# State space over spans of eight tokens, first norm in rows, and one reciprocal for sixteen heads' norms

## The reference

```python
h = rms_norm(x, mix_norm_g[layer])
proj = h @ w_in[layer]
u, q, k, v, f_logit, g_ssm, g_att = jnp.split(proj, IN_SPLITS, axis=-1)
y_ssm = s5_branch(u, ...)              # the state space
y_att = forgetting_attention(q, k, v, f_logit, ...)   # q and k get a norm per head
merged = jax.nn.sigmoid(g_ssm) * y_ssm + jax.nn.sigmoid(g_att) * y_att
x = x + merged @ w_out[layer]
```

```python
xr = jnp.einsum('blgh,gph->blgp', ug, br)     # and xi with bi
_, _, sr, si = lax.associative_scan(_complex_affine_combine, (lr, li, xr, xi), axis=1)
y = einsum(sr, c_re) - einsum(si, c_im) + d_skip * u
y = jax.nn.gelu(y); z = y @ w_glu             # then val * sigmoid(gate)
```

## Time and profile before

| | us |
|---|---|
| median of 3 runs | 4165.3 (4160.1 to 4167.3) |
| the profiled execution | 4165.7 |
| its span, first to last instruction | 4164.0 |
| PE busy | 3616.0 (87%) |
| GpSimd busy | 1846.4 (44%) |
| DVE busy | 2298.1 (55%) |
| ACT busy | 1454.7 (35%) |

### The profile page before, as it was taken

How to read it: one execution, slowest core, us unless ns; L and a number is a source line. 1 busy time by engine, 2 the same in 40 slices (tenths; PEclk the granted TensorE clock), 3 DMA queues, 4 the chain that set the end, 5 groups by cost and what they waited for, 6 DMA issues and landing times. The chain is left out here.

```text
span 4164.0 us, 51122 instructions
## 1 busy us (share of the span) xinstructions
PE 3616.0 (87%) x16437; PEld 2823.8 (68%) x16441; DVE 2298.1 (55%) x3833; ACT 1454.7 (35%) x2639; POOL 1846.4 (44%) x994
## 2 busy tenths in 40 slices
PE   7679889555699999999998885899998779989998
PEld 4546677445588888888887553668776554457876
DVE  5977325886498989898994357421102335531101
ACT  5124433177533333333332232433212114433322
POOL 1522342199787888788882110124342200024432
PEclk9889999767799999999999897999998869999999
DMA  3121232012577777777772110123223120012321
GB/s 88 51 73 27 58 97 73 11 81 98 194 267 267 268 267 271 268 265 264 268 272 66 53 42 26 31 66 95 78 83 77 52 77 19 8 56 86 94 76 62
DMA packets 430783, 486.52 MB, mean 117 GB/s; under 512 B 61344, under 2 KB 373952, under 8 KB 412496
## 3 DMA queue, kind: packets, MB, share of 16 engines
q1 hardware_dynamic: 412240, 350.98, 28.3%
q0 software_dynamic: 18432, 134.23, 8.1%
HBM read 448.35 MB, written 29.36 MB: 115 GB/s over the span
## 5 line engine op out<-in xcount | busy, mean ns | idle before, releaser
L124 POOL TENSOR_TENSOR w_low<-w_ring,w_high 128x1024 fp32r<-128x1024 f32 (+2 forms) x264 | 647.6, 2460 | 1675.9 <-ACT w_high L119 1675.9
L135 PE MATMUL ps<-h_low,w_high 128*128 128x512 f32 x1600 | 653.5, 408 | 161.1 <-POOL w_low L124 129.8
L136 PE MATMUL ps<-h_high,w_high 128*128 128x512 f32 x1600 | 640.0, 400 | 0.0
L137 PE MATMUL ps<-h_high,w_low 128*128 128x512 f32 x1600 | 638.7, 399 | 0.0
L135 PEld LDWEIGHTS ps<-h_low,w_high 128*128 128x128 f32 x1600 | 306.9, 192 | 255.6 <-POOL w_low L124 145.3
L124 POOL TENSOR_TENSOR u_low<-w_ring,u_high 128x1024 fp32r<-128x1024 f32 x128 | 366.4, 2862 | 136.8 <-ACT u_high L119 136.3
L119 ACT ACTIVATE w_high<-w_ring 128x1024 fp32r<-128x1024 f32 (+2 forms) x264 | 263.1, 1012 | 301.1 <-PE ps L137 254.1
L124 POOL TENSOR_TENSOR v_low<-v_raw,v_high 128x1024 fp32r<-128x1024 f32 x128 | 348.8, 2725 | 43.2 <-ACT v_high L119 43.2
L136 PEld LDWEIGHTS ps<-h_high,w_high 128*128 128x128 f32 x1600 | 307.4, 192 | 72.3 <-issue 3.6
L137 PEld LDWEIGHTS ps<-h_high,w_low 128*128 128x128 f32 x1600 | 306.7, 192 | 72.8
L135 PE MATMUL ps<-h_low,u_high 128*128 128x384 f32 x1024 | 345.1, 337 | 5.8 <-POOL u_low L124 5.8
(11 more groups left out here) (406 smaller groups left out, 7165.1 us busy)
## 6 DMA issues: line engine op xcount, KB each, us to landing
w_ring<-in_peer_uT_dram SPq DMA_DIRECT2D x128, 512.0 KB, 7.6
v_raw<-in_peer_uv_dram SPq DMA_DIRECT2D x128, 512.0 KB, 4.5
peer_gates<-ring SPq DMA_DIRECT2D x12, 2048.0 KB, 6.2
gates<-peer_gates SPq DMA_DIRECT2D x32, 768.0 KB, 9.5
w_ring<-in_ffn_w_gate_dram SPq DMA_DIRECT2D x44, 512.0 KB, 3.8
w_ring<-in_ffn_w_up_dram SPq DMA_DIRECT2D x44, 512.0 KB, 3.8
w_ring<-in_w_in_dram SPq DMA_DIRECT2D x36, 512.0 KB, 3.9
w_ring<-in_ffn_w_down_dram SPq DMA_DIRECT2D x32, 448.0 KB, 3.7
```

Source lines behind the costliest of these rows:

```text
L124: return eng.tensor_tensor(rounded(low), whole, high, ALU.subtract)
L135: nc.tensor.matmul(out, rounded(w_high), rounded(x_low), start=start, stop=False, **more)
L136: nc.tensor.matmul(out, rounded(w_high), rounded(x_high), start=False, stop=False, **more)
L137: return nc.tensor.matmul(out, rounded(w_low), rounded(x_high), start=False, stop=stop, **more)
```

## The change

The state space works on spans of eight tokens. u is copied out by phases (token mod 8), stored to DRAM and read back so that one partition range holds eight phases of a group's 16 channels. Three kinds of product take the place of fill and read-out over 512 tokens: `reachT` carries the eight inputs of a span into its state, a Toeplitz matrix (`toeplitz`, with the skip on its diagonal) gives what inputs of a span do to outputs of the same span, and `carry` gives what the state before the span does. The scan runs over 64 spans in six levels, all pairs at once. The tables are made by DVE from powers 0 to 8 of lambda. y leaves through DRAM and comes back in phases, and merge reads it by a strided view.

`project` gets a hook `between`: work of an engine after a given turn of its loop. Fill stands after turn 0, the band's DMAs (issued by ACT) after turn 3, read-out and gelu after turn 5. `load_consts` is gone; its loads stand first in the new stage `entry`, whose norm works on x in rows (one sum and one scale per partition). `c.xT` is made after the u projection from the rows and stays in place. The heads' norm gathers its 16 sums in 16 rows of one bank, takes one root and one reciprocal of 16x512, and spreads each row over 128 partitions by a product of halves.

The diff, cut to its core:

```diff
-def project(c, w, evacuate, rhs=None, ahead=None, whole=None, before={}, after={}, norm=None):
+def project(c, w, evacuate, rhs=None, ahead=None, whole=None, before={}, after={}, norm=None, between={}):
...
+    def pieces(eng, name, body, last):
+        at = 0
+        for stop in sorted(between):
+            turn_loop(eng, body, at, stop)
+            if name in between[stop]:
+                between[stop][name](eng)
+            at = stop
+        turn_loop(eng, body, at, last)
...
+    def square(self, act):
+        for t in range(TT):
+            act.wait_ge(self.x_in[t], 16)
...
+            self.c.nc.scalar.activation(self.squares, self.rows[:, t, :], ACT.Square, accum_out=self.total[:, t:t + 1]).then_inc(self.squared, 1)
...
+    def sum(self, pe):
+        pe.wait_ge(self.masks_set, 2)
+        spin(self.c, 7, 16)
...
+        for k in range(KD):
+            if k >= 4:
+                pe.wait_ge(self.low, k - 3)
+            for t in range(TT):
+                tr = self.c.nc.tensor.transpose(self.c.ps[:, 4 + k % 4, t * P:(t + 1) * P], self.scaled[:, t, k * P:(k + 1) * P], self.c.ident[:, :])
+            tr.then_inc(self.turned, 1)
...
+        def load_first(sp):
+            sp.dma_start(c.ident[:, :], c.ins["c_ident"]).then_inc(consts_in, 16)
+            sp.dma_start(c.causal[:, :], c.ins["c_causal"]).then_inc(consts_in, 16)
+            for two in range(2):
+                sp.dma_start(m["dt"][two * SSM_S:(two + 1) * SSM_S, :], dt2[two].partition_broadcast(SSM_S), allow_slow_non_contiguous=True).then_inc(param_in, 16)
+            sp.dma_start(m["ar"][:, :], by_state(A["ssm_a_re"][0]), allow_slow_non_contiguous=True).then_inc(param_in, 16)
+            sp.dma_start(m["ai"][:, :], by_state(A["ssm_a_im"][0]), allow_slow_non_contiguous=True).then_inc(param_in, 16)
+            norm.load_x(sp)
+            for x, name in enumerate(("ssm_b_re", "ssm_b_im")):
+                sp.dma_start(b_in[x][:, :, :], A[name][0].rearrange("(j two) s h -> (two s) j h", two=2)).then_inc(rows_in, 16)
...
+        def turn(pe):
+            for n in range(GROUPS):
...
+        def store_u(sp):
+            for b in range(SSM_T):
+                sp.wait_ge(u_out, b + 1)
+                sp.dma_start(u_dram[b, :, :], tb.phases[:, b, :]).then_inc(u_saved, 16)
+            sp.wait_ge(u_saved, 16 * SSM_T)
+            by_group = u_dram.rearrange("t (g h) (r s) -> r h (t g) s", h=SSM_H, r=PH)
+            for r in range(PH):
+                at = (PH - 1 - r) * SSM_H
+                sp.dma_start(tb.u[at:at + SSM_H, :, :], by_group[r]).then_inc(tb.u_in, 16)
...
+        def fill(pe):
+            pe.wait_ge(tb.u_in, 16 * PH)
+            for x in range(2):
+                for p in range(PAIRS):
+                    for two in range(2):
+                        mm = nc.tensor.matmul(c.ps[HALF[two], 2 + 2 * x + p // 8, p % 8 * SPANS:(p % 8 + 1) * SPANS],
+                                              tb.reachT[:, x, p, HALF[two]], tb.u[:, 2 * p + two, :], start=True, stop=True)
...
+            for p in range(PAIRS):
+                for x in range(2):
+                    for two, half in enumerate(HALF):
+                        mm = nc.tensor.matmul(c.ps[:, 6 + two, p * SSM_H:(p + 1) * SSM_H], tb.reach[half, x, p, :], tb.c[x][half, p, :], start=x == 0, stop=x == 1)
...
+        def band(act):
+            act.wait_ge(cleared, 1)
+            act.wait_ge(diagonal, 2)
+            for r in range(PH):
+                at = (PH - 1 - r) * SSM_H
+                act.dma_start(tb.toeplitz[at:P, r, :], tb.kernel[0:P - at, :, :].rearrange("p h g -> p (h g)")).then_inc(banded, 16)
+
+        def outputs(pe):
+            pe.wait_ge(banded, 16 * PH)
...
+            for p in range(PAIRS):
...
+                for two in range(2):
+                    g = 2 * p + two
+                    nc.tensor.matmul(out[two], toeplitz[:, g::SSM_G], tb.u[:, g, :], start=True, stop=False, skip_group_check=True)
+                for x in range(2):
+                    for two, half in enumerate(HALF):
+                        mm = nc.tensor.matmul(out[two][:, 1:SPANS], carry[half, x, p, :], tb.S[x][half, p, 0:SPANS - 1], start=False, stop=x == 1, skip_group_check=True)
...
+        def load_y(sp):
+            sp.wait_ge(y_saved, 16 * 4)
+            by_channel = y_dram.rearrange("(r h) (t g) s -> g t h r s", h=SSM_H, g=8)
             for g in range(8):
...
+                for t in range(SSM_T):
+                    sp.dma_start(ygT[g * SSM_H:(g + 1) * SSM_H, t, :].rearrange("p (r s) -> p r s", r=PH), by_channel[g, t]).then_inc(yg_in, 16)
...
         def sweeps(dve):
...
+            for x, (first, second, op) in enumerate((((0, 0), (1, 1), ALU.add), ((1, 0), (0, 1), ALU.subtract))):
+                step.mark(v.tensor_tensor(made[x], taps[first[0]], power[first[1]], ALU.mult))
+                step.mark(v.tensor_tensor(part, taps[second[0]], power[second[1]], ALU.mult))
+                step.wait()
+                step.mark(v.tensor_tensor(made[x], made[x], part, op))
+                step.wait()
...
-            for first in range(0, PAIRS, TOGETHER):
-                dve.wait_ge(moved, 2 * (first + TOGETHER))
-                for level in range(BIG):
-                    pair_steps(first, level, False)
...
+            dve.wait_ge(moved, 4)
+            for level in range(LEVELS):
                 all_step(level, False)
...
+            dve.wait_ge(kernel_out, 2)
+            v.memset(tb.toeplitz, 0.0).then_inc(cleared, 1)
...
+        project_copy(c, w_qk, qkT, ahead, before={"dve": sweeps}, after={"sp": load_y},
+                     between={1: {"pe": fill, "act": move}, 4: {"act": band}, 6: {"pe": outputs, "act": gelus}})
...
-                nc.vector.reciprocal(rstd[:, n % ring, :], rstd[:, n % ring, :]).then_inc(inverted, 1)
...
+            v.reciprocal(rstd[:, :], rstd[:, :]).then_inc(inverted, 1)
...
+                v.scalar_tensor_tensor(buf[:, n, :], buf[:, n, :], gains[:, n:n + 1], c.ps[:, wide_banks[n % len(wide_banks)], :], ALU.mult, ALU.mult).then_inc(normed, 1)
```

More of the change, by code:

```diff
@@ L203, in sem @@
         return self.sems[-1]
[L206 to L241, removed]
-            @block.scalar
-            def _(act):
-                for k in range(KD):
-                    act.wait_ge(transposed, k + 1)
-                    nc.scalar.activation(c.xT[:, k, :], c.ps[:, k, :], ACT.Copy).then_inc(copied, 1)
-                act.wait_ge(copied, KD)
 class Norm:
@@ L404, in _ @@
                     ahead.load(c, sp, 0, b)
+            if "sp" in after:
+                after["sp"](sp)
         @block.gpsimd
         def _(pool):
+            if "pool" in before:
+                before["pool"](pool)
             def body(i):
@@ L525, in tile_of, with project_copy @@
     return buf[:, i * per_turn + b, :]
-def project_copy(c, w, dest, ahead=None, before={}, after={}, norm=None):
+def project_copy(c, w, dest, ahead=None, before={}, after={}, norm=None, between={}):
     nc = c.nc
@@ L536, in act @@
             split(b)
-    project(c, w, {"act": act}, ahead=ahead, before=before, after=after, norm=norm)
+    project(c, w, {"act": act}, ahead=ahead, before=before, after=after, norm=norm, between=between)
 def project_add(c, w, dest, rhs, whole=None, ahead=None, before={}):
@@ L1204, in ssm, with entry @@
+def entry(c, A, tb, w_u, w_qk, room):
     nc = c.nc
     with c.stage() as ctx:
[L1206 removed]
+        names = ("ar", "ai", "dt", "mag", "th", "turn", "cos", "sin", "lre", "lim", "nr", "den", "cre", "cim", "t0", "t1", "half_pi")
         PM = [P, PAIRS]
[L1208 to L1212 removed]
@@ new lines, in entry @@
+        m = {n: ctx.sbuf(n, PM) for n in names}
+        b_in = [ctx.sbuf(f"b_in{x}", [P, PAIRS, SSM_H]) for x in range(2)]
+        tmp = tb.tmp
+        wide = [ctx.sbuf(f"wide{x}", [P, 4, PAIRS]) for x in range(2)]
+        rows, scaled = (room[:, at:at + KD, :].rearrange("p (t two) n -> p t (two n)", two=2) for at in (0, KD))
+        norm = EntryNorm(c, ctx, A["mix_norm_g"][0], rows, scaled, tb.product[:, 0:KD, :].rearrange("p q n -> p (q n)"))
+        u_dram = nc.dram_tensor("u_phases", (SSM_T, P, T), F32).ap()
@@ new lines, in turn @@
+        def turn(pe):
+            for n in range(GROUPS):
+                if n >= 4:
+                    pe.wait_ge(moved, n - 3)
+                if n == KD + 8:
+                    pe.wait_ge(c_in, 16 * 5)
+                if n in (KD, KD + 4):
+                    pe.wait_ge(reached, (n - KD) // 4 + 1)
+                for y in range(4):
+                    if n < KD:
+                        source = rows[:, y, n * P:(n + 1) * P]
+                    elif n < KD + 8:
+                        source = tb.reach[:, (n - KD) // 4, 4 * ((n - KD) % 4) + y, :]
+                    else:
+                        source = tb.c_rows[n - KD - 8][:, y, :, :].rearrange("p two s -> p (two s)")
+                    tr = nc.tensor.transpose(c.ps[:, 4 + n % 4, y * P:(y + 1) * P], source, c.ident[:, :])
```

(7 more changed lines are left out.)

555 lines of the change are left out of this document (326 added, 229 removed).

## The result

The changed kernel takes 4140.78 us (median of five runs, 4134.59 to 4143.76) against 4165.19 us (4160.13 to 4167.31, five runs too): the ratio is 0.9941, with a 95% interval of 0.9926 to 0.9955. Forecast were 57 us, measured are 24.4. The profiled execution has a span of 4139.0 us, against 4164.0.

The account below looks back on a forecast made before the run. DVE, busy 190 of 204 us, was taken to bound the scan's stage. Through the scan -58.5 us (entry's +5.5 included), heads' norm +0.5 and merge +1 gave -57 from 4165.3: 4108 us, range 4090 to 4129.

Parts of the forecast that it names:

- Entry: Load, first norm and u: `dt` loads close SP's queue some 19 us; +5.5 us (0 to +12).
- rival B: Entry: `dt` does not close the queue in its new place, entry 16 us shorter: 4092 us; chance 0.05.
- First tiles, fill, sweeps: Scan's start: turn 0 to 101.9, fill 12.5 us (7 to 25), all-pairs sweeps 44 us, diagonal done at 159.
- The new wait: Scan, after turn 3: ACT waits for DVE's diagonal, then issues the band; PE stands 7.5 us ahead of turn 5.
- Read-out: Scan, after turn 5: 96 small products at 95 ns each, 10 us (6 to 20).
- Rival C: Scan: small products at half clock (12 us more), GpSimd starved beside carry (5 us more): 4125 us; chance 0.19.
- Rival E: Scan: all-pairs sweeps take twice as long beside GpSimd, ACT waits 40 us more: 4148 us; chance 0.04.
- Rival D: Scan: 224 small products at 0.40 us, weight load and product each exposed, +68 us: 4176 us; chance 0.03.
- small products over 0.2 us apart: Scan's fill and read-out: a named sign that the forecast, which took 95 ns a product, is wrong.
- The stage's end: End of scan: 32 loads of y behind the next weights make SP end the stage at 222.5, 10 us after PE.
- Heads' norm and merge: After the scan: heads' norm +0.5 us (-1 to +4), merge's strided reading +1 us (0 to +3).

Follow-up runs that it names:

- e5: The changed kernel with the two `dt` loads issued by ACT instead of SP, nothing else moved: 4133.95 us.
- e9: The changed kernel with `dt` in one load of 128 rows of 128 bytes, ACT picking every second step: 4121.76 us.
- e1: The changed kernel with the band laid out group by group, so a Toeplitz product's 128 weight columns are neighbours: 4140.19 us.
- e3: The changed kernel with neighbouring Toeplitz weight columns and a 512-column product ahead of each pair of the read-out: 4129.44 us.
- e2: The changed kernel with one unused bf16 product of 512 columns ahead of each of the read-out's 16 pairs: 4119.34 us.
- e4: The changed kernel with SP's 32 loads of y issued ahead of the next stage's weight loads: 4127.72 us.
- e7: The changed kernel with the heads' norm of the kernel before, all else unchanged: 4131.41 us.
- e12: The changed kernel with an extra bf16 product of only 64 columns ahead of each pair of the read-out: 4138.87 us (one run).
- e11: The changed kernel with one `dt` load, y loads ahead, wide products in read-out and fill, and a wait for ACT's first copy: 4109.07 us.

## Why the prediction was wrong, step by step

**Entry: right, its reason half right.** +4.1 against +5.5. The loads of `dt` do hold everything for 19 us, x is issued at 23.3 and the trigonometry starts at 25.9, near what was worked out. Behind that two errors cancel: the first product of u came at 48.3 and not at 46, and u took 22 us (its last copy begins at 70.4) where the sum had 26.7 (its 46 + 26.7 is 72.7, not 72). Nor do the `dt` loads close SP's queue alone: moved to ACT's queue they hold SP as long (e5). What fits both is one DMA engine that they fill, through which others must go as well. Against rival B (`dt` doesn't hold x in its new place) the traces speak plainly; the 16 us that it had promised came only in e9, with another load.

**First tiles, fill, sweeps: right, the fill by luck (see the read-out).** Turn 0 ends at 100.8 (forecast 101.9), fill takes 13.3 us (12.5), DVE's diagonal is done at 151.9 (159). The product of 128x2048 was 2.29 us alone (2.3), and 4.4 beside GpSimd.

**The new wait: it did not reach PE.** ACT issues the band for 6.2 us (0.78 each, where I had 0.45) and its copy waits behind it. But DVE was 7 us sooner than forecast, and a difference of two long chains takes such an error whole: ahead of turn 5 PE did not stand at all instead of 7.5 us, and turn 5 ended at 174.1, not 180. The 1.13 us that it did stand come earlier and are GpSimd's. With issues of 16 us the forecast wait is there: 7.1 us in e1 and 9.5 in e3, both ahead of turn 5.

**Read-out: the step that failed.** Forecast 10 us (6 to 20), measured 32.4: 22 of the 32 missing us. The term is mis-sized three times over, as the experiments take it apart. 16 pairs at 1.18 us, neighbouring weights and full clock, are 18.9 us: this is the plain price, 0.29 us for a product over 128 rows and 0.15 for one over 64, where I took 0.095. Strided weights add 16 x 0.42 = 6.7 us, which makes 25.6; e2 ran at 25.7. Half clock adds 16 x 0.51 = 8.2 us on that, which makes 33.8 (32.4 were measured, since the first pairs still ran at full clock), and 2.4 us on the tiles behind it (25.0 us to the last copy, 22.6 in e2).

The 0.095 was wrong from the start: it divides the time by the records, and a product of this kind leaves two. The code of L2590 has 4 tiles x 16 heads, 64 products for the x128 of the earlier trace rows, and L2568 has 16 products for x32. So the rows say 0.19 and 0.23 us a product, not 0.096 and 0.114. Their windows in the kernel before, first of L2568, then of L2590:

```profile
3359.45:3363.00 3.55, 3.55 (x34) 3.55 (x32) 0.00 (x0) 1.80 (x3) 0.00 (x0) 1.00 0.00 0
...
3375.00:3378.00 3.00, 3.00 (x32) 3.00 (x32) 1.75 (x4) 0.63 (x1) 0.00 (x0) 0.50 0.00 0
```

The second shows half clock with PE busy for the whole window, in a run of nothing but small products: what cost the read-out 8 us could be read there. Counted as products, 32 at 0.23 and 64 at 0.19 are 19.5 us, at the end of the range given for this term. The rest is form: the rows were products over 64 rows with 32 columns and products with one column; neither had 128 rows and 64 columns, and none had strided weights.

In the fill the wrong price came out right by luck: 64 products over 128 rows with only 64 weight columns took 4.0 us, 0.06 each, and the 64 over 64 rows with 16 columns 9.4, 0.15 each and in part at half clock.

Rival C had the slow clock, but for 12 us and with a cause in PE standing; here PE did not stand from 151.4 on, and its clock was 1.00 from 160 to 170. Its time, 4125, is 16 us low, since price and clock came together. Rival E's 4148 is nearer, but its mechanism isn't there: the sweeps were early. Rival D had the price, 0.40 us for every small product and 0.36 as the point from which it decides; the read-out's 96 cost 0.34 each, the fill's 128 only 0.10. It had been given 0.03. Of the signs of being wrong that were named, "small products over 0.2 us apart" is the one that came.

**The stage's end: right.** SP's last load of y is issued 10.8 us behind PE's last tile, forecast 10 (205.3 + 1 + 16 is 222.3, not 222.5); e4 removes it and gains 10.6.

**Heads' norm and merge: right.** +0.1 by e7 where 0.5 was forecast (the marks have +1.5); merge's first product comes 10.7 us behind ACT's first split instead of 9.4, +1.3 where +1 was forecast.

**Not foreseen: what later stages lose.** Between the start of the heads' stage and the end the difference shrinks by 13.5 us (38.6 to 25.1), of which 1.5 was forecast. The marks give 1.5 to the heads' stage, 2.9 to attention, where rows show the clock, 1.4 to merge's start, 1.2 from there to the next norm and 6.6 to all that follows. Of this last part, in stages of equal code, 3.3 lie where the rows show a lower clock; that single stages turn on the clock by 8 us is shown by the rows of e2, but those large turns are not between before and after. The range, 39 us wide, had no term for it. With the read-out at its forecast size the time would have been about 4118, within the range but not at the 4108 forecast; what stays open is why the clock comes back early in one kernel and late in another.

## What to carry to other kernels

Count products in the code and not records in the trace before dividing. Then price a small fp32 product by a row with its own rows and columns, and if the trace has none, let the range reach to the form that is worst in each of rows, stride and clock. A run of nothing but small products dropped TensorE to half clock here while the engine was never idle; a wide product hidden behind a weight load kept the clock up in one such run and not in another. When a transfer of a few KB takes 20 us, look at the DMA share beside it and at its pieces: reading whole rows and picking the wanted elements on chip took 16 us off the start.

## What was not expected of the hardware

- Two loads of 1024 pieces of 4 bytes, at a DMA share of 0.05 and 0.07 (about one engine in sixteen), held up loads on their own queue and, in e5, on another one: `ai` landed 22.2 us after its issue in e5, and 4.7 us in e9, with the same 2048 pieces of its own.
- The granted clock fell from 1.00 to 0.50 while PE was 10.00 of 10 us busy, with small products only. In the read-out it stayed at 1.00 with one wide product in 1.61 us (e2) or 1.30 us (e3), and fell with a narrow one (e12); in the fill it fell with one wide product in 1.32 us too (e11). The Trainium skill (TensorE: Matmul & The Clock Gate, section "HAM oscillation — how this bites in real kernels") tells of a fall behind pauses of PE; the rows of the read-out show one without a pause.
- Strided weights, every 32nd fp32 column, cost 0.21 us a product at full clock and nothing at half clock.
- Eight DMA issues on ACT took 6.2 us with rows of 2048 bytes and 16.4 us with pieces of 64 bytes, and all that time ACT did nothing else.
